# A two-block model on one core: when the S5 state chain, its Toeplitz matrices and the two normalisations run beside the RWKV scan

## The chip, the cores and the metric

One core of a Trainium2 chip runs the whole program. The metric is device time in microseconds (us) of one launch. The names of the engines in the profile are: PE (TensorE, matrix products), DVE (VectorE), ACT (ScalarE), POOL (GpSimd) and SP (SyncE, which here only issues DMA transfers).

## The reference, cut to what matters

The input `x` has 512 tokens of 1024 features. The first block mixes two recurrences, and the change lies in this block only:

```
h = modulate(rms_norm(x), sh_m, sc_m)
proj = h @ w_in[l]                      # z (RWKV columns) and u (S5 columns)
y_rwkv = rwkv7_time_mix(z, ...)         # S = S*w + (S a) b + v k ;  y = S r ; group norm, gate
y_s5 = s5_mix(u, ...)                   # diagonal complex state space, gelu, GLU, rms norm
mix = jnp.concatenate([y_rwkv, y_s5], axis=-1) @ w_out[l]
x = x + g_m[:, None, :] * mix
h = modulate(rms_norm(x), sh_f, sc_f)
x = x + g_f[:, None, :] * ((silu(h @ ffn_w_gate[l]) * (h @ ffn_w_up[l])) @ ffn_w_down[l])
...
```

Inside `s5_mix`, the state of each of 32 groups of 16 channels obeys `s_t = abar * s_(t-1) + bbar u_t`, the output is `Re(C s) + d u`, then `zz = gelu(y)`, `out = zz * sigmoid(zz @ w_glu + b_glu)`, and an rms norm. After this block come two layers of a hybrid of latent attention, short convolution and windowed attention.

## The kernel before, in words

Everything is kept feature-major in SBUF, 128 features by 512 tokens per tile. A dense product takes its weights as blocks of 128x128 in the order in which PE uses them: eight blocks are one unit, 512 KB. SP loads units into a ring of four (`Sync.load`), ACT rounds a unit to its high part (`Scalar.unit`), DVE computes the low part (`Vector.unit`), and PE does three matmuls for each block (`mms`). Two units are split ahead at most. The units of the `ada` product (a vector times a matrix) are used raw from the ring, eight matmuls for four units: SP loads unit u+4 when PE has used unit u (`Sync.whole_done`).

Each engine's program is written by hand as a set of Python generators, one for each strand of the work: `z` (the input projection), `p` (preparation of RWKV), `m` (S5 matrices), `s` (the S5 strand, `s5_apply`), `r` (the RWKV strand), `a` (columns of ada), `g` (group norm) and `o` (first part of the output product). Two strings, `PREP` and `MIX` at the top of the file, set the order: `play` reads a string and takes one step of the named generator for each letter. All engines read the same strings, so a yield that is added to a strand on one engine has to be added on the others. An engine works through its program in order; only semaphores tie the engines together.

The RWKV strand has these steps: token-major v; the grams of `m` and `mt` (two steps); for each of four pairs of chunks p the grams `G` (`grams`) and the token-major b and k; `a` and `kav`; the inverse, five levels of eight steps (four times P: PE 16 matmuls of 64x64, ACT copies; four times T: PE 32 matmuls of 64x64, DVE adds; POOL masks `LL` for the next level); the step matrices (`steps`: four MW, four PR); and eight steps of the scan S0 to S7. In each scan step PE needs the state that DVE scaled in the step before.

The S5 strand has these steps. SP writes u to DRAM and fetches it back with groups on partitions (`UG`). PE computes the local inputs E, ACT copies them to `S`. DVE then runs the state chain: seven steps within blocks of eight (i1 to i7, in `PREP`), seven steps over the block ends (b1 to b7, five operations on 128x32 or 128x16 each), and two steps, called rest 0 and rest 1 here, of four operations on 128x784. The signal `states` stands at their end. SP fetches the Toeplitz matrices `TT` from DRAM with eight DMAs of 256 KB (L3049), PE computes Y in two halves (16 matmuls with `TT` and 32 with `S` each), ACT copies it to `UG`, SP writes it to DRAM with eight DMAs (`scr_yd`, L3056), reads it back as `YS` (L3062) and fetches x once more (L3063). DVE, ACT and DVE again turn `YS` into gelu and its high and low parts (`skip`, `hi`, `lo`), PE computes four `glu` tiles, and the S5 norm gives the rows 4 to 7 of the output product's input (`os`, then `hi` on ACT and `lo` on POOL). Group norm gives rows 0 to 3. `begin_outs` computes a part of the first four output tiles, and `out_one` the rest, 35 us of dense matmuls.

Before the change, the place of the S5 strand is this: b1 to b7 in one step right behind the first grams mask; rest 0 and rest 1 among the grams G0 and G1; the TT fetch on SP behind `states`; the two halves of Y within level 1 of the inverse; `skip` within level 3; `glu` between the steps of the scan; the S5 norm ahead of group norm; and `begin_outs` with rows 4 to 7.

```
for b in range(1, 8):
    step(Sv[:, :, :, b, 7], Sv[:, :, :, b - 1, 7], ...)
yield
...
self.wait_ge(k.s("kpad", 16), "k")
self.wait_ge(k.s("s5_dve"), "states")
for t in range(8):
    self.e.dma_start(k.TT[16 * t:16 * t + 16, :, :], ...)
```

Of the kernel before, what the change touches and what calls it, by code (L numbers as in the profile page):

```python
# [13 lines left out]
T = 512  # L14
# [10 lines left out]
PREP = "zpzzpz" + "smzpm" + "szpmzp" + "ssss" + "zps" + "zpss" + "zpss" + "zps" + "zps"  # L25
MIX = ("rrsrrsrrsrrrsrarrra" + "rrrrrra" + "rrrrsrrsa" + "rrrrrrsa" + "rrrrrrrra" + "rrrsrrrra" + "rrrrrrr" + "rrrrarrrr"
       + "ras" + "rs" * 6 + "r" + "gogoogo")
# [354 lines left out]
class Tensor(Engine):  # L382
# [229 lines left out]
    def s5_apply(self):  # L612
# [16 lines left out]
        for _ in range(11):  # L629
            yield  # L630
        for half in range(2):
            qs = (2 * half, 2 * half + 1)
            ps = [self.take(("yg", q)) for q in qs]
            self.wait_ge(k.s("tt", 16), 7)
            self.wait_ge(k.s("s5_dve"), "states")
            for i in range(8):
                for par in (0, 1):
                    g = 2 * (8 * half + i) + par
                    self.mm(ps[par][:, i * 64:i * 64 + 64], k.TT[:, g, :], k.UG[:, g, :], i == 0, False)
            for i in range(8):  # L640
                for ri in range(2):
# [22 lines left out]
        self.give("s5norm", (act, "ln"))  # L664
        yield
# [49 lines left out]
    def grams(self):  # L715
# [21 lines left out]
        for p in range(4):  # L737
            for which in (0, 1):
# [8 lines left out]
                for hp in (0, 1):  # L747
                    self.give(("g", p, hp, which), (dve, ("g", p, hp, which)))
# [191 lines left out]
    def begin_outs(self):  # L940

        k = self.k
        late = [[(k.s("gn_act"), ("hi", r)), (k.s("gn_pool"), ("lo", r))] for r in range(4, 8)]
        for n in range(4):
            self.begin_out("out", n, k.ysp[4:], range(4, 8), late)
            yield

    def out_one(self):
# [3 lines left out]
        for n in range(8):  # L952
            if n < 4:
                self.dense(("out", n), [("out", n, r) for r in range(4)], k.ysp[:4], k.bank["out", n][:, :], each[:4],
# [291 lines left out]
class Vector(Engine):  # L1246
# [345 lines left out]
    def s5_apply(self):  # L1592
# [4 lines left out]
        yield  # L1597
        for _ in range(4):
# [26 lines left out]
        yield  # L1625
        T = [k.region(110 + 3.125 * i, 16, 7, 7) for i in range(4)]
        ends = [Sv[:, ri, :, 0:7, 7].unsqueeze(3).broadcast_to((128, 16, 7, 7)) for ri in (0, 1)]
        power = lambda ap: ap[:, 0:7, :].rearrange("p i g -> p g i").unsqueeze(2).broadcast_to((128, 16, 7, 7))
        self.wait_ge(k.s("s5_pe"), ("e", 1, 1))
        for ri, op in ((0, ALU.subtract), (1, ALU.add)):  # L1630
            rest = Sv[:, ri, :, 1:8, 0:7]
            V(T[2 * ri], ends[ri], power(k.P8R), ALU.mult)
            V(T[2 * ri + 1], ends[1 - ri], power(k.P8I), ALU.mult)
            self.wait_ge(dve, SOFAR)
            V(rest, rest, T[2 * ri], ALU.add)
            self.wait_ge(dve, SOFAR)
            V(rest, rest, T[2 * ri + 1], op, *(["states"] if ri else []))
            yield
        for _ in range(4):
# [12 lines left out]
        for n in range(4):  # L1652
# [3 lines left out]
            yield  # L1656
        rr = k.rtmp[:, 2, :].rearrange("p (t j) -> p t j", t=8)
# [60 lines left out]
    def grams(self):  # L1718
# [13 lines left out]
        for p in range(4):  # L1732
            for which in (0, 1):
                for hp in (0, 1):
# [3 lines left out]
                    self.tt(part(k.KA if which else k.LT), pv[:, :, 0, :], mask("mSU"), ALU.mult).then_inc(  # L1738
                        *dve.inc(("l", p, hp, which)))
# [374 lines left out]
class Scalar(Engine):  # L2114
# [191 lines left out]
    def s5_apply(self):  # L2306
# [11 lines left out]
        for _ in range(11):  # L2318
            yield
        for q in range(4):  # L2320
            g0 = 16 * (q // 2) + q % 2
# [78 lines left out]
    def rwkv(self):  # L2400
# [16 lines left out]
        self.wait_ge(k.s("prep_dve"), ("bv", 3))  # L2417
        for p in range(4):
            yield
# [324 lines left out]
class Pool(Engine):  # L2744
# [29 lines left out]
    def s5_apply(self):  # L2774
        k = self.k
        for _ in range(2 + 4 + 11 + 2 + 2 + 1 + 4 + 1):
# [6 lines left out]
    def rwkv(self):  # L2783
# [15 lines left out]
        for p in range(4):  # L2799
            self.wait_ge(gdve, ("l", p, 1, 0))  # L2800
# [138 lines left out]
class Sync(Engine):  # L2939
# [90 lines left out]
    def s5_apply(self):  # L3030
# [13 lines left out]
        for _ in range(10):  # L3044
            yield
        self.wait_ge(k.s("kpad", 16), "k")
        self.wait_ge(k.s("s5_dve"), "states")
# [4 lines left out]
        for _ in range(2):  # L3052
# [187 lines left out]
```

## Time and profile before

| | us |
|---|---|
| median of 3 runs | 1702.82 (1700.56 to 1703.16) |
| the profiled execution's own time | 1701.19 |
| its span, first to last instruction | 1699.4 |
| PE busy | 1519.1 (89%), at a mean granted clock of 0.938 |
| DVE busy | 801.0 (47%) |
| ACT busy | 578.9 (34%) |
| POOL busy | 268.3 (16%) |

Busy shares are averages over stages with different limits. In the profile, a wait of an engine is shown as idle time with the engine or transfer that ended it; "issue" means that nothing in the profile ended it. The granted clock is 1.00 at 2.4 GHz and 0.50 at 1.2 GHz.

### The profile page before, as it was taken

How to read it: one execution, taken by the hardware profiler on the slowest of the kernel's cores; microseconds unless marked ns; L12 is line 12 of the kernel's file. 1: busy time of each engine (PE TensorE's matmuls, PEld its weight loads, DVE VectorE, ACT ScalarE, POOL GpSimd, SP SyncE). 2: the span in 40 equal slices, each digit the busy share in tenths (PEclk: the TensorE clock that was granted, in tenths of full speed). 3: DMA queues.
4: the chain of work that ended last, by engine and by line, in shares of the span. 5: the costliest groups of instructions: out<-in, count | busy, mean ns of one | idle time of the engine just before them, and what ended most of it. 6: DMA issues, size and time to landing. Idle time of an engine off the chain costs nothing.

```text
span 1699.4 us, 23751 instructions
## 1 busy us (share of the span) xinstructions
PE 1519.1 (89%) x10024; PEld 1179.0 (69%) x10024; DVE 801.0 (47%) x1264; ACT 578.9 (34%) x996; POOL 268.3 (16%) x224
## 2 busy tenths in 40 slices
PE   6898668788889999999979899988898999998989
PEld 3676548667568888888866687756686677766767
DVE  7666931242554233232345545446634455445552
ACT  4365121123523222222224434224522444222441
POOL 0000312200101011100002233232201232222220
PEclk9999877878889999999989999999998999999999
DMA  9251072731122232332221121111123111211121
GB/s 364 68 121 59 20 127 75 231 145 39 40 72 88 99 98 88 99 130 87 100 88 50 38 75 62 62 50 38 62 88 105 38 54 58 75 62 38 50 87 62
DMA packets 51897, 144.17 MB, mean 85 GB/s; under 512 B 13264, under 2 KB 18000, under 8 KB 51024
## 3 DMA queue, kind: packets, MB, share of 16 engines
q1 hardware_dynamic: 51792, 142.65, 26.1%
q8 instruction: 80, 1.31, 0.3%
q14 instruction: 25, 0.20, 0.0%
HBM read 137.95 MB, written 4.69 MB: 84 GB/s over the span
## 4 chain that ended last, share of the span: by engine, by line
PE 71%; DVE 13%; ACT 8%; issue 4%; DMA 2%; POOL 1%; SPq 1%; DVEq 0%; ACTq 0%
PE b L392 70%; ACT arena L2121 4%; DVE arena L1250 3%; DVE arena L1258 2%; DVE ring L1250 2%; PE b L395 1%; DVE X L1250 1%; ACT ring L2124 1%; POOL arena L2751 1%; DVE arena L1951 1%; DMA ring<-in_ws 1%; ACT L2121 1%; ACT arena L2124 1%; DVE arena L2084 1%; ACT tile L2124 1%
## 5 line engine op out<-in xcount | busy, mean ns | idle before, releaser
L392 PE MATMUL b<-tile,ring 128*128 128x512 f32 x2288 | 705.0, 403 | 9.1 <-DVE ring L1250 5.1
L392 PE MATMUL b<-HR,ring 128*128 128x512 f32 (+1 forms) x1888 | 624.2, 407 | 62.7 <-DVE ring L1250 34.7
L392 PEld LDWEIGHTS b<-tile,ring 128*128 128x128 f32 x2288 | 436.6, 191 | 115.0 <-issue 8.2
L392 PEld LDWEIGHTS b<-HR,ring 128*128 128x128 f32 (+1 forms) x1888 | 364.3, 193 | 164.0 <-issue 61.4
L1250 DVE TENSOR_TENSOR ring<-ring,ring 128x1024 fp32r<-128x1024 f32 x186 | 254.9, 1372 | 299.8 <-ACT ring L2124 295.9
L2124 ACT ACTIVATE ring<-ring 128x1024 fp32r<-128x1024 f32 x186 | 195.7, 1054 | 214.7 <-PE b L392 214.7
L392 PE MATMUL b<-arena 64*64 64x64 f32 (+10 forms) x3072 | 230.8, 290 | 37.9 <-issue 16.7
L392 PEld LDWEIGHTS b<-arena 64*64 64x64 f32 (+5 forms) x3072 | 147.4, 151 | 111.2 <-issue 74.5
L2124 ACT ACTIVATE arena<-b 128x512 f32<-128x512 f32 (+2 forms) x138 | 75.5, 569 | 259.2 <-PE b L392 195.5
L1250 DVE TENSOR_TENSOR arena<-arena 128x512 f32<-128x512 f32 (+7 forms) x194 | 100.3, 549 | 80.0 <-ACT arena L2121 59.1
L2751 POOL TENSOR_SCALAR arena<-arena 128x128 f32<-128x128 f32 (+1 forms) x64 | 87.0, 1378 | 208.9 <-DVE arena L1956 208.9
L2748 POOL TENSOR_TENSOR tile<-arena,tile 128x512 fp32r<-128x512 f32 x38 | 49.8, 1315 | 441.4 <-ACT tile L2124 441.4
L2121 ACT ACTIVATE arena<-arena 128x512 f32<-128x512 f32 (+7 forms) x151 | 72.7, 501 | 84.7 <-DVE arena L1254 46.0
L1250 DVE TENSOR_TENSOR arena<-b,arena 128x512 f32<-128x512 f32 (+3 forms) x78 | 47.8, 629 | 111.9 <-PE b L392 110.6
L2748 POOL TENSOR_TENSOR arena<-arena 128x256 f32<-128x256 f32 (+3 forms) x60 | 64.5, 1098 | 176.3 <-DVE arena L2093 88.3
L395 PE MATMUL b<-cst,arena 128*128 128x128 f32 (+1 forms) x520 | 68.5, 285 | 18.0 <-DVE arena L1250 6.9
L2121 ACT ACTIVATE arena<-b,arena 128x512 f32<-128x512 f32 (+1 forms) x80 | 43.9, 558 | 112.8 <-DVE arena L1254 108.4
L395 PEld LDWEIGHTS b<-cst,arena 128*128 128x128 f32 (+1 forms) x520 | 61.6, 143 | 29.8 <-issue 17.8
L2124 ACT ACTIVATE tile<-arena 128x512 fp32r<-128x512 f32 x58 | 35.2, 628 | 137.9 <-DVE arena L1250 117.5
L1250 DVE TENSOR_TENSOR arena<-arena,b 128x512 f32<-128x512 f32 x52 | 33.5, 681 | 93.1 <-PE b L392 93.0
L392 PE MATMUL b<-ring,HR 128*128 128x512 f32 (+1 forms) x256 | 64.5, 344 | 1.7 <-DVE arena L1261 1.2
L2121 ACT ACTIVATE arena<-b,par 128x512 f32<-128x512 f32 (+1 forms) x58 | 37.5, 685 | 68.2 <-PE b L392 41.4
(112 smaller groups left out, 1024.5 us busy)
## 6 DMA issues: line engine op xcount, KB each, us to landing
ring<-in_ws SPq DMA_DIRECT2D x218, 512.0 KB, 3.5
arena<-in_ws SPq DMA_DIRECT2D x15, 512.0 KB, 15.2
arena<-in_lw SPq DMA_DIRECT2D x2, 1280.0 KB, 5.5
X<-in_xT SPq DMA_DIRECT2D x2, 1024.0 KB, 6.1
arena<-scr_kpad SPq DMA_DIRECT2D x8, 256.0 KB, 11.9
X<-in_xT SPq DMA_DIRECT2D x1, 2048.0 KB, 13.7
outT<-X SPq DMA_DIRECT2D x8, 256.0 KB, 2.0
arena<-in_cst SPq DMA_DIRECT2D x1, 1088.0 KB, 5.1
```

The costliest lines, as they stand in the source:

```text
L392: return self.e.matmul(out, lhsT, rhs, start=start, stop=stop, skip_group_check=True)
L395: return self.e.transpose(out, in_, self.k.C("ident"))
L1250: return self.e.tensor_tensor(out=out, in0=a, in1=b, op=op)
L1258: return self.e.scalar_tensor_tensor(out=out, in0=a, scalar=s, in1=b, op0=op0, op1=op1)
L1951: self.e.tensor_reduce(out=mx[:, q:q + 1], in_=ps[:, o:o + n], op=ALU.max, axis=AX.X).then_inc(*dve.inc((l, "max", h, q)))
L2084: self.e.tensor_reduce(out=mx, in_=Z[:, :, lo:256], op=ALU.max, axis=AX.X).then_inc(*dve.inc((l, "wmax", n)))
L2121: return self.e.activation(out, a, f, scale=scale, **kw)
L2124: return self.e.activation(out, a, ACT.Copy)
L2748: return self.e.tensor_tensor(out=out, in0=a, in1=b, op=op)
L2751: return self.e.tensor_scalar(out=out, in0=a, scalar1=s1, scalar2=None, op0=op0)
```

## The change

It moves steps of the S5 strand and changes no arithmetic. The parts are:

1. SP fetches `TT` right behind E (it waits for `("e", 1, 1)` of PE in the place of `states`), in `PREP`.
2. The block ends b1 to b7 become seven steps of their own, and stand with rest 0 and rest 1 in the levels 1 to 4 of the inverse. Rest 0 and rest 1 use two temporaries at 52 KB in the place of four at 110 KB, which `TT` now fills, so they wait for the last P of level 4.
3. The masking of `LT` on DVE becomes a plain copy on ACT (`gram_act`): the level masks on POOL are strict enough.
4. The two halves of Y move from level 1 of the inverse to the steps PR0 to PR3, each half in two steps (with `TT`, and with `S`).
5. `skip` moves behind scan step S4, `glu` behind S6 and between the steps of group norm, and the S5 norm behind the second step of group norm.
6. `begin_outs` takes the rows 0 to 3 (RWKV), and `os`, `hi` and `lo` of rows 4 to 7 come behind it.
7. The groups of ada stand a little differently among the steps.

```diff
-PREP = "zpzzpz" + "smzpm" + "szpmzp" + "ssss" + "zps" + "zpss" + "zpss" + "zps" + "zps"
-MIX = ("rrsrrsrrsrrrsrarrra" + "rrrrrra" + "rrrrsrrsa" + "rrrrrrsa" + "rrrrrrrra" + "rrrsrrrra" + "rrrrrrr" + "rrrrarrrr"
-       + "ras" + "rs" * 6 + "r" + "gogoogo")
+PREP = "zpzzpz" + "smzpm" + "szpmzp" + "sssss" + "zps" + "zpss" + "zpss" + "zps" + "zps"
+MIX = ("rrrrarrrrarrrrr" + "rrrrrrrra" + "rrsrrsrrrra" + "rrsrrsrrrra" + "rrsrrsrrsrra" + "rrrrsrrsrra"
+       + "rrrrrsrsarsrs" + "rarsrrrsrsrsr" + "sgssgsg" + "oooo" + "s")
...
             ps = [self.take(("yg", q)) for q in qs]
             self.wait_ge(k.s("tt", 16), 7)
-            self.wait_ge(k.s("s5_dve"), "states")
             for i in range(8):
                 for par in (0, 1):
                     g = 2 * (8 * half + i) + par
                     self.mm(ps[par][:, i * 64:i * 64 + 64], k.TT[:, g, :], k.UG[:, g, :], i == 0, False)
+            yield
+            self.wait_ge(k.s("s5_dve"), "states")
...
-        late = [[(k.s("gn_act"), ("hi", r)), (k.s("gn_pool"), ("lo", r))] for r in range(4, 8)]
+        early = [[(k.s("gn_act"), ("hi", r)), (k.s("gn_dve"), ("lo", r))] for r in range(4)]
         for n in range(4):
-            self.begin_out("out", n, k.ysp[4:], range(4, 8), late)
+            self.begin_out("out", n, k.ysp[:4], range(4), early)
             yield
...
-                self.dense(("out", n), [("out", n, r) for r in range(4)], k.ysp[:4], k.bank["out", n][:, :], each[:4],
+                self.dense(("out", n), [("out", n, r) for r in range(4, 8)], k.ysp[4:], k.bank["out", n][:, :], each[4:],
                            start=False)
...
         for b in range(1, 8):
             step(Sv[:, :, :, b, 7], Sv[:, :, :, b - 1, 7], ...)
-        yield
-        T = [k.region(110 + 3.125 * i, 16, 7, 7) for i in range(4)]
+            yield
+        T = [k.region(52 + 3.125 * i, 16, 7, 7) for i in range(2)]
...
-        self.wait_ge(k.s("s5_pe"), ("e", 1, 1))
+        self.wait_ge(k.s("inv_pe"), ("p", 4, 3))
...
-                    self.tt(part(k.KA if which else k.LT), pv[:, :, 0, :], mask("mSU"), ALU.mult).then_inc(
-                        *dve.inc(("l", p, hp, which)))
+                    if which:
+                        self.tt(part(k.KA), pv[:, :, 0, :], mask("mSU"), ALU.mult).then_inc(*dve.inc(("l", p, hp, which)))
...
+            for hp in (0, 1):
+                self.wait_ge(k.s("gram_dve"), ("g", p, hp, 0))
+                self.cp(k.LT[:, p, :].rearrange("p (n a t) -> p n a t", a=2, t=64)[:, :, hp, :],
+                        k.bank["g", p, hp, 0][:, :].rearrange("p (n a t) -> p n a t", a=2, t=64)[:, :, 0, :]).then_inc(
+                    *gram.inc(("l", p, hp)))
...
-            self.wait_ge(gdve, ("l", p, 1, 0))
+            self.wait_ge(k.s("gram_act"), ("l", p, 1))
...
-        for _ in range(10):
-            yield
         self.wait_ge(k.s("kpad", 16), "k")
-        self.wait_ge(k.s("s5_dve"), "states")
+        self.wait_ge(k.s("s5_pe"), ("e", 1, 1))
         for t in range(8):
             self.e.dma_start(k.TT[16 * t:16 * t + 16, :, :], ...)
         yield
-        for _ in range(2):
+        for _ in range(7 + 7 + 2 + 4):
             yield
```

The other lines of the diff only add or drop yields so that the strand keeps step on every engine.

SP's queue from the fetch of `UG` (X<-scr_ud) to the re-read of x. Line numbers grow by 12 to 15 through the change. Before:

```order
17 L3039 DMA X<-scr_ud 16x32x64 x8
18 L2944 DMA ring<-in_ws 128x1024 x6
19 L2983 DMA arena<-in_small 128x512
20 L3049 DMA arena<-scr_kpad 16x32x128 x8
21 L2944 DMA ring<-in_ws 128x1024 x16
22 L3056 DMA scr_yd<-X 16x32x64 x8
23 L3058 DMA arena<-scr_ud 128x4x512
24 L2944 DMA ring<-in_ws 128x1024 x8
25 L3062 DMA arena<-scr_yd 128x4x512
```

And now:

```order
17 L3053 DMA X<-scr_ud 16x32x64 x8
18 L2958 DMA ring<-in_ws 128x1024 x2
19 L3061 DMA arena<-scr_kpad 16x32x128 x8
20 L2958 DMA ring<-in_ws 128x1024 x4
21 L2997 DMA arena<-in_small 128x512
22 L2958 DMA ring<-in_ws 128x1024 x32
23 L3068 DMA scr_yd<-X 16x32x64 x8
24 L3070 DMA arena<-scr_ud 128x4x512
25 L3074 DMA arena<-scr_yd 128x4x512
```

The `TT` fetch (from `scr_kpad`) moved ahead of four weight loads; all loads for ada now stand ahead of the write of `yd`, and none between it and its re-read.

DVE from the last gram masks (arena<-b,cst) into the inverse (adds are arena<-arena,b 128x512, the block ends are the rows with X and 32 or 16 columns). Before:

```order
191 L1250 TENSOR_TENSOR arena<-b,cst 128x4x64 x8
192 L1250 TENSOR_TENSOR arena<-X,arena 128x784 x2
193 L1250 TENSOR_TENSOR X<-X,arena 128x16x7x7 x2
194 L1250 TENSOR_TENSOR arena<-b,cst 128x4x64 x16
195 L1250 TENSOR_TENSOR arena<-arena,b 128x512 x4
196 L1250 TENSOR_TENSOR ada<-b,par 128x8
197 L1250 TENSOR_TENSOR arena<-arena,b 128x512 x12
```

And now:

```order
165 L1253 TENSOR_TENSOR arena<-b,cst 128x4x64 x24
166 L1253 TENSOR_TENSOR arena<-arena,b 128x512 x8
167 L1253 TENSOR_TENSOR ada<-b,par 128x8
168 L1253 TENSOR_TENSOR arena<-X,arena 128x32 x2
169 L1253 TENSOR_TENSOR X<-X,arena 128x32
170 L1253 TENSOR_TENSOR X<-X,arena 128x16 x2
171 L1253 TENSOR_TENSOR arena<-X,arena 128x32 x2
...
193 L1253 TENSOR_TENSOR arena<-arena,b 128x512 x4
194 L1253 TENSOR_TENSOR arena<-X,arena 128x784 x2
195 L1253 TENSOR_TENSOR X<-X,arena 128x16x7x7 x2
196 L1253 TENSOR_TENSOR arena<-arena,b 128x512 x2
```

The masks are now in one piece of 24 instead of 8, 8 and 16, and the block ends and the two rests lie between adds of the inverse.

DVE in the scan (states are arena<-b,nst 128x256), as it now stands:

```order
217 L1253 TENSOR_TENSOR arena<-b,nst 128x256 x4
218 L1261 SCALAR_TENSOR_TENSOR arena<-arena,par 128x512 x4
219 L1253 TENSOR_TENSOR tile_70<-arena,tile_69 128x512
220 L1253 TENSOR_TENSOR tile_72<-arena,tile_71 128x512
221 L1253 TENSOR_TENSOR tile_74<-arena,tile_73 128x512
222 L1253 TENSOR_TENSOR tile_76<-arena,tile_75 128x512
223 L1253 TENSOR_TENSOR arena<-b,nst 128x256
224 L1253 TENSOR_TENSOR ring_55<-ring,ring_55 128x1024 x2
225 L1253 TENSOR_TENSOR arena<-b,nst 128x256
```

`skip` (row 218) and the four `lo` now stand between the states of S4 and S5; before they stood in level 3 of the inverse.

## Rows read from the trace of the kernel before

**Rows 1.** Windows: us, busy us (x instructions) of PE, PEld, DVE, ACT, POOL, PEclk, DMA share, GB/s

```profile
186.10:252.80 66.70, 41.66 (x784) 31.61 (x784) 39.36 (x90) 11.72 (x20) 18.54 (x12) 0.77 0.49 73
252.80:376.60 123.80, 100.61 (x2385) 88.99 (x2388) 33.54 (x59) 26.50 (x45) 20.09 (x16) 0.81 0.44 148
376.60:455.70 79.10, 66.58 (x872) 49.84 (x864) 29.37 (x47) 32.19 (x49) 4.95 (x4) 0.87 0.15 51
455.70:491.20 35.50, 35.38 (x144) 28.07 (x144) 16.97 (x22) 11.58 (x15) 0.00 (x0) 0.95 0.28 90
```

**Rows 2.** Timeline of PE, grams to level 0: start, us, what, count, [idle before <-releaser]

```profile
203.68 1.97 PE L395 MATMUL b<-cst,arena 128*128 128x128 f32 x8 [6.92 <-DVE arena L1250]
...
216.32 1.99 PE L392 MATMUL b<-arena 64*64 64x128 f32 x32 [6.15 <-DVE arena L1250]
...
223.85 1.98 PE L392 MATMUL b<-arena 64*64 64x128 f32 x32 [2.49 <-DVE arena L1250]
...
243.43 1.76 PE L392 MATMUL b<-H,arena 64*64 64x64 f32 x27 [7.24 <-issue]
246.24 6.67 PE L392 MATMUL b<-ring,nst 128*32 128x512 f32 x16 [1.05 <-DMA ring<-in_ws]
```

**Rows 3.** Timeline of POOL (first row) and DVE, 192 to 259 us

```profile
192.25 5.01 POOL L2748 TENSOR_TENSOR arena<-arena,cst 128x512 f32<-128x512 f32 x4 [141.73 <-DVE arena L1250]
...
193.73 3.57 DVE L1250 TENSOR_TENSOR X<-X,arena 128x32 f32<-128x32 f32 x3
...
197.70 0.54 DVE L1250 TENSOR_TENSOR X<-X,arena 128x32 f32<-128x32 f32 x3
...
217.43 2.94 DVE L1250 TENSOR_TENSOR arena<-X,arena 128x784 f32<-128x784 f32 x2
220.39 1.98 DVE L1250 TENSOR_TENSOR X<-X,arena 128x784 f32<-128x784 f32 x2
...
257.80 1.28 DVE L1250 TENSOR_TENSOR arena<-arena,b 128x512 f32<-128x512 f32 x2 [30.13 <-PE b L392]
```

**Rows 4.** Timeline of SP's queue: the TT fetch and the write of yd

```profile
222.46 9.51 SPq L3049 DMA_DIRECT2D arena<-scr_kpad  x8
...
300.16 10.23 SPq L3056 DMA_DIRECT2D scr_yd<-X  x8
```

**Rows 5.** Waits of PE with no releaser, 159 to 456 us: total, times, longest

```profile
PE b L392 <- issue: 27.9, 9, 7.2
```

**Rows 6.** Timeline of PE, Y and two groups of ada

```profile
271.57 14.09 PE L392 MATMUL b<-X,arena 128*128 128x64 f32 x96
...
289.00 7.50 PE L392 MATMUL b<-X,arena 128*128 128x64 f32 x96
296.43 1.94 PE L392 MATMUL b<-ring,nst 128*32 128x512 f32 x16
...
348.46 3.90 PE L392 MATMUL b<-ring,nst 128*32 128x512 f32 x16 [6.01 <-DVE arena L1250]
```

**Rows 7.** Windows around the first half of Y, columns as in rows 1

```profile
271.00:286.00 15.00, 15.00 (x120) 14.70 (x122) 0.00 (x0) 0.89 (x2) 1.27 (x1) 0.52 0.01 2
```

**Rows 8.** Landing of the eight writes of yd (source line L3056)

```profile
DMA to landing us min/median/max: 3.5/5.9/6.5
```

**Rows 9.** Chain that ended last: the re-read of yd (start, us, what)

```profile
331.86 9.43 DMA arena<-scr_yd
```

**Rows 10.** DMA issues on the page: the re-read of x (KB, us to landing)

```profile
X<-in_xT SPq DMA_DIRECT2D x1, 2048.0 KB, 13.7
```

**Rows 11.** Timelines of DVE, PE and POOL: lo, os, group norm's first products, lo of POOL

```profile
345.27 2.50 DVE L1250 TENSOR_TENSOR tile<-arena,tile 128x512 fp32r<-128x512 f32 x4 [1.22 <-ACT tile L2124]
...
421.32 4.00 DVE L1258 SCALAR_TENSOR_TENSOR arena<-arena,par 128x512 f32<-128x512 f32 x4 [6.84 <-ACT arena L2121]
...
427.87 5.76 PE L392 MATMUL b<-arena,cst 128*128 128x512 f32 x8 [1.12 <-ACT arena L2124]
...
426.07 4.95 POOL L2748 TENSOR_TENSOR tile<-arena,tile 128x512 fp32r<-128x512 f32 x4 [92.32 <-ACT tile L2124]
```

More of the change, by code:

```diff
@@ L628, in s5_apply @@
                 yield
-        for _ in range(11):
+        for _ in range(1 + 7 + 7 + 2):
             yield
@@ L747, in grams @@
                 for hp in (0, 1):
-                    self.give(("g", p, hp, which), (dve, ("g", p, hp, which)))
+                    self.give(("g", p, hp, which), (dve, ("g", p, hp, which)),
+                              *([] if which else [(k.s("gram_act"), ("l", p, hp))]))
             yield
@@ L1597, in s5_apply @@
         yield
+        yield
         for _ in range(4):
@@ L1624, in s5_apply @@
                  k.P8I[:, 7, :].unsqueeze(1).broadcast_to((128, 2, 16)), T[0][:, :, :, 0], T[1][:, :, :, 0])
-        yield
-        T = [k.region(110 + 3.125 * i, 16, 7, 7) for i in range(4)]
+            yield
+        T = [k.region(52 + 3.125 * i, 16, 7, 7) for i in range(2)]
         ends = [Sv[:, ri, :, 0:7, 7].unsqueeze(3).broadcast_to((128, 16, 7, 7)) for ri in (0, 1)]
         power = lambda ap: ap[:, 0:7, :].rearrange("p i g -> p g i").unsqueeze(2).broadcast_to((128, 16, 7, 7))
-        self.wait_ge(k.s("s5_pe"), ("e", 1, 1))
+        self.wait_ge(k.s("inv_pe"), ("p", 4, 3))
         for ri, op in ((0, ALU.subtract), (1, ALU.add)):
             rest = Sv[:, ri, :, 1:8, 0:7]
-            V(T[2 * ri], ends[ri], power(k.P8R), ALU.mult)
-            V(T[2 * ri + 1], ends[1 - ri], power(k.P8I), ALU.mult)
             self.wait_ge(dve, SOFAR)
-            V(rest, rest, T[2 * ri], ALU.add)
+            V(T[0], ends[ri], power(k.P8R), ALU.mult)
+            V(T[1], ends[1 - ri], power(k.P8I), ALU.mult)
             self.wait_ge(dve, SOFAR)
-            V(rest, rest, T[2 * ri + 1], op, *(["states"] if ri else []))
+            V(rest, rest, T[0], ALU.add)
+            self.wait_ge(dve, SOFAR)
+            V(rest, rest, T[1], op, *(["states"] if ri else []))
             yield
-        for _ in range(4):
+        for _ in range(4 + 1):
             yield
@@ L1656, in s5_apply @@
             yield
+        yield
         rr = k.rtmp[:, 2, :].rearrange("p (t j) -> p t j", t=8)
@@ L2317, in s5_apply @@
                 yield
-        for _ in range(11):
+        for _ in range(1 + 7 + 7 + 2):
             yield
         for q in range(4):
+            if q % 2 == 0:
+                yield
             g0 = 16 * (q // 2) + q % 2
@@ L2417, in rwkv @@
         self.wait_ge(k.s("prep_dve"), ("bv", 3))
+        gram = k.s("gram_act")
         for p in range(4):
+            for hp in (0, 1):
[3 more added lines that the diff above has]
+                    *gram.inc(("l", p, hp)))
             yield
@@ L2775, in s5_apply @@
         k = self.k
-        for _ in range(2 + 4 + 11 + 2 + 2 + 1 + 4 + 1):
+        for _ in range(2 + 4 + 1 + 7 + 7 + 2 + 4 + 2 + 1 + 4 + 1):
             yield
```

## The prediction

> **What bounds the kernel now.** I read the page first: PE is busy 89% of the span, but the change touches only a part of it, so next came the windows of that part [rows 1]. Behind 491.2 us nothing changes, and ahead of 186.1 us only the fetch of TT moves. Between them PE idles 25.0 us in the grams (66.70 less 41.66), 23.2 us in inverse and step matrices (123.80 less 100.61) and 12.5 us in the scan and group norm. The granted clock is 0.77 to 0.87 there against 0.95 in the dense stage behind, so idle time is paid a second time in slow matmuls.
>
> The timelines tell what ends those waits. In the grams PE waits 6.92, 6.15 and 2.49 us for DVE [rows 2], whose queue holds the block ends and the two rests among the masks [rows 3]. Then it stops for 7.24 us with no releaser, and its next ada weights come late [rows 2]: SP issued the TT fetch only when `states` was there, for 9.51 us [rows 4]. In the whole stretch PE has nine waits with no releaser, 27.9 us [rows 5]; they lie in streams of 64x64 matmuls while DMA moves much data, so I read them as instructions that come late. In the inverse the first half of Y ran 14.09 us and the second 7.50 us for the same 96 records [rows 6], the first at clock 0.52 [rows 7]; and PE waited 6.01 us for `skip`, behind which ada ran 3.90 us in the place of 1.94 us [rows 6].
>
> **Stage 1, 186.1 us to the first P of the inverse (now 252.8).** The block ends, the rests and one third of the masks leave DVE. PE's three waits for it go: -15.6 us. Each pair of chunks now needs six masks on DVE and 2.5 us of grams on PE, so DVE keeps up, but banks come free in turn: I put back 2. The TT fetch leaves: the stop of 7.24 us shrinks to an ordinary one of 3.4 (the other eight average 2.6, the longer ones are 3.4), -3.8; the late weights go, 1.05 of waiting and 6.67 down to 1.94 [rows 2, 6], -5.8. The eight transposes behind the first wait ran at the low clock, 1.97 us [rows 2]; warm they take about half: -0.9. The loads behind the first ada group, which were held back until now, can cost one more stop: +3.4. Sum -20.7, bounds -26 (no added stop, no wait for banks) and -13 (both PE waits come back in half).
> The copy of LT on ACT costs nothing: ACT is busy 11.72 of 66.70 us [rows 1]. If that cover were gone, POOL's level masks would be late, and PE's first P with them.
>
> The TT fetch itself, earlier on, stands ahead of weight loads. SP is taken for 9.51 us and the transfers fill the DMA engines for some 17 to 19 us. A load is wanted four units after it is allowed, each of 24 matmuls of 0.246 us (35.38 / 144 [rows 1]), less some 2.4 us for splitting, so 21 us; 9.5 of it in the queue still leave 11. I cost it at 0; if that cover is gone, it costs PE at most 4 us once.
>
> **Stage 2, to the first scan step (now 376.6).** Y no longer runs cold: its halves should take 7.2 us each in the place of 14.09 and 7.50: -7.2 [rows 6]. The wait for `skip` goes, -6.0, and the cold stretch behind it, -5.5 (ada 2.0, its sums 1.6, the rest of the level 2). The block ends fall where DVE idles: it sat 30.13 us before level 0 [rows 3], and each level leaves it some 3 us and each ada group 2 to 4 more; a step takes 0.9 us (0.54 us [rows 3] for its last three operations, and some 0.4 for the first two). Beside POOL it does not: the three took 3.57 us [rows 3]. I cost them at 0 since they start while PE is at ada; at the other end, seven times 3.0, +21. The rests do cost. They start with the last P; rest 0 takes 4.9 us (2.94 and 1.98 [rows 3]), two adds 1.3, rest 1 4.9, one add 0.7: 11.8 us until the third MW may start, while PE has only T (2.1), ada with its sums (3.9) and two MW (3.5): +2.4. One more us for the Y steps among PR. Sum -15.3, bounds -25 and +6. With stage 1 the scan starts at 376.6 - 36.0 = 340.6 us.
>
> **Stage 3, the scan to the first dense end (now 491.2).** Here the change gives back. The chain of the S5 output starts with the scan and nothing of `glu` can stand in for it. From the start of S0: copies of Y 1.3 us; eight writes of yd, 10.23 us of issue [rows 4] and up to 6.5 to land [rows 8], 16.0; the re-read 0.6 and 7. It took 9.43 behind weight loads [rows 9]; now none stands in front, but x still shares with it (13.7 us [rows 10]); bounds 4 and 13.7. Then `skip`, gelu, hi and lo, 6.4 us (341.31 to 347.7, its last row [rows 11]). That is 31.3 us, and DVE cannot give the state of S5 before, since `skip` stands ahead of it. PE has six scan steps of some 2 to 3 us and one sum, 18 us: **it stands still for about 13 us**. Then S6 and the first glu at the low clock, S7 and the second glu, 11.8; the means 3.7; two glu 6.1; variances 3.6. ACT makes the roots ahead of the last square of the S5 norm, so PE idles 5 and ends that norm at 63.3 us; first gate 0.9, and DVE's four times 2.17 us and one low, so the first row of the output is ready at 72.4 us. As a check: means to first output row took 455.7 - 427.9 = 27.9 us before [rows 11], and take 28.7 here.
> Then the four begun tiles, 12.3 us, to 84.7. Behind the second of them the next unit's split holds DVE until 80.8; `os` 4.00, `hi`, then POOL 4.95 [rows 11] give the last row at 90.7: +4.2. The rest is the 35.4 us of before [rows 1]. Sum 124.3 us against 114.6: +9.7, bounds +2 and +20.
>
> **Sum.** -20.7 - 15.3 + 9.7 = -26.3 us on the profiled execution: 1701.19 - 26.3 = 1674.9. The median of the runs shown lies 1.6 us above that execution, so 1676.5, and I say **1677 us**.
>
> What could speak against it is a rule. The trace shows the stop of 7.24 us inside a stream of matmuls, while 512-byte pieces of TT fill the DMA engines [rows 2, 4]. The Trainium skill (Runtime: NRT & Kernel Launch, section Instruction fetch mechanics) says that instructions are fetched in blocks of 16 KiB while the block before runs, and that this is mostly hidden. If the stop has another cause, it stays, and the sum is 3.8 us smaller: 1681. I go by the row.
>
> **Rivals.**
> *Warm tail (0.20).* The re-read lands in 4 us and the writes of yd, with no weight loads beside them, in 10; the last rows are ready in time; one stop less. That is 3 + 6 + 4 + 3 us more: 1661. For it: nothing else is in the DMA queues. Against: the pieces of yd are 256 bytes.
> *Cold middle (0.24).* Stops of 3.4 us behind every ada group stay [rows 5], and the clock falls behind them and behind the wait for the rests, so that Y keeps its 7.2 us and the levels 5 more, and the block ends meet POOL once: 1677 + 7 + 5 + 3 = 1692. For it: rows 7.
> *Late re-read, slower (0.04).* One mechanism, at DVE's `skip` between the states of S4 and S5: everything behind it moves one for one with the landing of the re-read. It lands 24.9 us after S0 starts by my sum; the gain is used up at 24.9 + 26 = 51 us. The nearest rows reach that only if all queue up: weight loads of ada 14, writes of yd 16.7, x ahead of the re-read 13.7 and the re-read itself 9.4, 54 us: 1706. Against it: SP waits for yd before it issues either, and issues the re-read first.
> *No change (0.02).* The two gains only move PE's idle time to the wait in the scan.
>
> **How the numbers follow.** My forecast (1677, give or take 7) has 0.50. The range reaches to the centres of both neighbours: 1661 to 1693. About 0.2% (3.4 us) is what a measurement of this kernel can tell from no change; faster by more than that holds for the forecast and the first two rivals, 0.94; the same 0.02; slower 0.04.
>
> **What would show it.** Right: no wait of PE over 3 us for DVE between 190 us and the first P, which starts near 232; SP's TT fetch near 139 us, with no longer wait of PE for ring rows between 140 and 165; Y in four pieces at clock 1.00, 14 to 15 us in all; S0 near 341; a single wait of PE of 10 to 16 us in the scan, ended by DVE's state of S5, with the landing of the re-read ahead of it; and dense matmuls to the end from about 425. Wrong: Y at 20 us or more; waits of PE for DVE within the levels 1 to 3, next to slow operations on 128x32; or a wait in the scan over 25 us.

## The result and the profile after

The changed kernel takes 1654.88 us (median of 4 runs, 1654.14 to 1660.91) against 1701.69 (4 runs, 1700.43 to 1703.16): ratio 0.9732, 95% interval 0.9707 to 0.9757. Beside a later batch it took 1655.36 (6 runs), ratio 0.9721 (0.9697 to 0.9744). The direction was right, the size was not: forecast 1677, range 1661 to 1693.

Windows of the changed kernel, cut at the same places of the program as [rows 1]: grams, first P to S0, S0 to the last dense product of the output, the rest (us, then busy us and instructions of PE, PEld, DVE, ACT, POOL, then PEclk, DMA share, GB/s):

```profile
185.58:219.50 33.92, 32.73 (x784) 26.29 (x786) 16.92 (x39) 14.70 (x29) 14.93 (x12) 0.95 0.36 128
219.50:318.60 99.10, 85.65 (x2395) 73.89 (x2390) 51.84 (x100) 19.06 (x33) 20.05 (x16) 0.97 0.36 130
318.60:445.14 126.54, 106.28 (x1010) 81.83 (x1008) 50.54 (x67) 50.68 (x74) 4.97 (x4) 0.84 0.29 88
445.14:1659.00 1213.86, 1127.37 (x4984) 873.31 (x4984) 548.40 (x794) 410.30 (x748) 223.46 (x182) 0.96 0.22 72
```

| stage | before | after | difference | forecast |
|---|---|---|---|---|
| 1, grams | 66.70 | 33.92 | -32.8 | -20.7 |
| 2, first P to S0 | 123.80 | 99.10 | -24.7 | -15.3 |
| 3, S0 to the last dense product | 114.60 | 126.54 | +11.9 | +9.7 |

The rest took 1208.20 us before; its instructions are unchanged, and the profiled execution (1660.91 us) lies 6 us above the kernel's other three, so the last row is no part of the change.

PE in the grams: the waits for DVE and the stop of 7.24 us of [rows 2] are gone, and the 128 matmuls of `kav` (fifth row) run in one piece. The first group of ada takes 1.94 us, the second 4.30: its weights still arrive a little late (PE's own weight loads wait for `ring<-in_ws` twice within it), and with thin weights, below, it takes 1.95. Timeline (start, us, what, [idle before <-releaser]):

```profile
193.68 2.56 PE L392 MATMUL b<-arena 64*64 64x64 f32 x103 [1.19 <-issue]
196.17 1.94 PE L392 MATMUL b<-ring,nst 128*32 128x512 f32 x16
...
203.91 4.30 PE L392 MATMUL b<-ring,nst 128*32 128x512 f32 x16
...
212.09 3.71 PE L392 MATMUL b<-cst,arena 128*64 128x128 f32 x64
215.73 3.95 PE L392 MATMUL b<-H,arena 64*64 64x64 f32 x128
```

DVE: the last three operations of a block end, alone and beside POOL's masks, and the second rest (two multiplies, two adds):

```profile
233.51 0.54 DVE L1253 TENSOR_TENSOR X<-X,arena 128x32 f32<-128x32 f32 x3
...
234.45 3.58 DVE L1253 TENSOR_TENSOR X<-X,arena 128x32 f32<-128x32 f32 x3
...
287.69 2.98 DVE L1253 TENSOR_TENSOR arena<-X,arena 128x784 f32<-128x784 f32 x2
290.70 1.99 DVE L1253 TENSOR_TENSOR X<-X,arena 128x784 f32<-128x784 f32 x2
```

PE around the rests and Y: no wait for DVE stands in front of the MW at 290.47, and Y is four pieces of 3.79 us (the first two shown), 15.2 in all for the 21.6 of [rows 6]:

```profile
285.64 1.15 PE L392 MATMUL b<-arena 64*64 64x64 f32 x32 [1.47 <-issue]
286.72 1.94 PE L392 MATMUL b<-ring,nst 128*32 128x512 f32 x16
288.60 1.95 PE L392 MATMUL b<-cst,H 128*128 128x1 f32 x16
290.47 8.32 PE L392 MATMUL b<-arena 64*64 64x128 f32 x160
...
303.48 3.79 PE L392 MATMUL b<-X,arena 64*128 64x63 f32 x64
```

The S5 output chain (SP's queue; two pieces of the chain that ended last: the end of the last write and the re-read; DVE), then PE from the end of the scan: the state of S5, the first glu, the last square of the S5 norm, the gates, the begun tiles and the rest of the output:

```profile
319.80 8.04 SPq L3068 DMA_DIRECT2D scr_yd<-X  x8
...
326.53 4.15 DMA scr_yd<-X
...
330.70 8.22 DMA arena<-scr_yd
...
338.95 2.74 DVE L1261 SCALAR_TENSOR_TENSOR arena<-arena,par 128x512 f32<-128x512 f32 x4 [5.82 <-DMA arena<-scr_yd]
```

```profile
345.79 1.65 PE L392 MATMUL b<-arena 64*64 64x64 f32 x26 [1.41 <-DVE arena L1253]
349.40 4.67 PE L392 MATMUL b<-tile,ring 128*128 128x512 f32 x12
...
379.54 2.08 PE L392 MATMUL b<-arena,cst 128*128 128x512 f32 x2 [6.63 <-ACT arena L2127]
381.41 4.74 PE L392 MATMUL b<-arena 128*128 128x512 f32 x8
391.38 14.14 PE L392 MATMUL b<-tile,ring 128*128 128x512 f32 x48 [5.24 <-ACT tile L2130]
408.67 36.45 PE L392 MATMUL b<-tile,ring 128*128 128x512 f32 x144 [3.15 <-POOL tile L2762]
```

### The profile page after: what moved, and what is told of

Its sections match the earlier page's. It is cut to its first block, busy times and chain, and to the rows that moved or that the text cites. A ratio compares the mean times of both kernels' runs of the same rounds, so it can differ in the third digit from the quotient of the medians.

```text
span 1659.0 us, 23756 instructions
## 1 busy us (share of the span) xinstructions
PE 1502.9 (91%) x10024; PEld 1164.8 (70%) x10024; DVE 801.2 (48%) x1256; ACT 581.5 (35%) x1004; POOL 264.3 (16%) x224
## 3 DMA queue, kind: packets, MB, share of 16 engines
q8 instruction: 80, 1.31, 0.3%
## 4 chain that ended last, share of the span: by engine, by line
PE 73%; DVE 12%; ACT 8%; issue 4%; POOL 1%; DMA 1%; SPq 0%; DVEq 0%; ACTq 0%
PE b L392 72%; ACT arena L2127 5%; DVE arena L1261 2%; DVE ring L1253 2%; DVE arena L1253 2%; PE b L395 1%; ACT ring L2130 1%; POOL arena L2765 1%; DVE arena L1957 1%; DVE arena L2090 1%; ACT arena L2130 1%; ACT L2127 1%; DVE arena L1915 1%; ACT tile L2130 1%; DMA cst<-in_cst 1%
## 5 line engine op out<-in xcount | busy, mean ns | idle before, releaser
L392 PE MATMUL b<-tile,ring 128*128 128x512 f32 x2288 | 709.9, 405 | 13.5 <-ACT tile L2130 5.2
L2127 ACT ACTIVATE arena<-b 128x512 f32<-128x512 f32 (+1 forms) x44 | 24.7, 561 | 84.3 <-PE b L392 84.3
## 6 DMA issues: line engine op xcount, KB each, us to landing
arena<-in_ws SPq DMA_DIRECT2D x15, 512.0 KB, 15.2
arena<-scr_kpad SPq DMA_DIRECT2D x8, 256.0 KB, 11.8
X<-in_xT SPq DMA_DIRECT2D x1, 2048.0 KB, 12.7
```

What stands on the lines that cost most here:

```text
L392: return self.e.matmul(out, lhsT, rhs, start=start, stop=stop, skip_group_check=True)
L2127: return self.e.activation(out, a, f, scale=scale, **kw)
```

## The experiments

Each difference below is a median against the changed kernel's 1654.9 or 1655.4 us; ratios are against the kernel before, timed beside each batch. The changed kernel itself ran only beside three of them (thin weights, both tail edits, the tail's old order). The kernel before had medians from 1701.7 to 1704.9 us in these batches, so a difference of 3 to 5 us of the other runs is not clear of noise by the times alone; there the rows of the trace carry the reading.

### Which part of stage 1 gives what

**TT alone**: the kernel before with the `TT` fetch behind E; the rests' temporaries go to `H`, since `TT` fills theirs.

```diff
-        for _ in range(10):
-            yield
         self.wait_ge(k.s("kpad", 16), "k")
-        self.wait_ge(k.s("s5_dve"), "states")
+        self.wait_ge(k.s("s5_pe"), ("e", 1, 1))
         for t in range(8):
             self.e.dma_start(k.TT[16 * t:16 * t + 16, :, :], ...)
         yield
+        for _ in range(10):
+            yield
```

> The kernel before with one part of the change alone: SP fetches TT behind E (the two rests use two temporaries elsewhere, so nothing else moves). Theory W (my prediction's terms: a stop shrinks to an ordinary one of 3.4 us, the ada weights come in time): -3.8 - 5.8 = -9.6 us against before, so 1692. Theory C (a stop without a releaser is caused wholly by the transfer beside it and goes wholly, and the clock behind it stays high): -7.2 - 5.8 - 1 or more, so 1688 or less. Rival N (the fetch was hidden, or it takes the time again where it now lies, among the weight loads of the projection): 1699 or more.

Measured: 1688.35, ratio 0.9927 (0.9890 to 0.9964), 14 us faster, as theory C has it. The first P (the first product of the inverse) stands at 239.31 us for 252.84. PE's waits for DVE remain (7.12, 6.30 and 2.59 us); `kav` runs unbroken and ada behind it in 2.09 us:

```profile
229.66 3.71 PE L392 MATMUL b<-cst,arena 128*64 128x128 f32 x64
233.30 4.06 PE L392 MATMUL b<-H,arena 64*64 64x64 f32 x128
237.29 2.09 PE L392 MATMUL b<-ring,nst 128*32 128x512 f32 x16
239.31 3.89 PE L392 MATMUL b<-arena,ring2f 64*64 64x64 f32 x126
```

So the stop of 7.24 us went as a whole, not down to 3.4. Of the later ones the next, in level 0, is longer here, 2.58 us for 1.46. The stage from the first transposes to the first P, columns as in the windows above:

```profile
186.31:239.31 53.00, 35.94 (x785) 29.66 (x785) 39.54 (x90) 11.73 (x20) 17.58 (x12) 0.81 0.12 42
```

This run moves the stop and the late weights together and does not price the stop alone. In the kernel before, the chain that ended last runs between 225 and 246 us from SP's issue of TT over the weights of ada queued behind it, and not through the stop:

```profile
232.02 14.17 DMA ring<-in_ws
```

These weights were there only at 246.2 us. With the stop alone gone, PE would have waited for them as long.

**Block ends back**: the changed kernel with b1 to b7 and both rests among the grams again (the letters of `MIX` moved, temporaries in `H`).

> The changed kernel with the block ends and the two rests back among the grams on DVE (temporaries in a free place), all else as changed. Theory W: PE gets back its waits of 6.9, 6.2 and 2.5 us and nothing else, +15.6 against the changed kernel, so 1670.5. Theory C: beside these waits the clock falls, which makes the matmuls of the grams some 5 us longer, so 1675 or more. Rival I (in the inverse they cost time as well, beside POOL): under +12, so under 1667.

Measured: 1667.90, ratio 0.9793 (0.9753 to 0.9833), +13.0, between theory W and rival I. First P at 233.14 for 219.50. The waits are not those of the kernel before: 6.99, 3.16 and 0.79 us, with the copies of `LT` on ACT. The first two:

```profile
203.60 3.66 PE L392 MATMUL b<-ring,nst 128*32 128x512 f32 x16 [6.99 <-DVE arena L1253]
...
215.45 2.90 PE L392 MATMUL b<-arena 64*64 64x128 f32 x64 [3.16 <-ACT arena L2130]
```

**TT among the grams**: the changed kernel with the fetch between the loads for two groups of ada.

> The changed kernel with the TT fetch put back among the grams, behind the masks of G0 and ahead of the loads for the next ada group. Theory W: a stop of 3.8 us and late weights of 5.8 us come back, +9.6, so 1664.5. Theory C: the whole stop of about 7 us and the late weights, and cold matmuls behind both, so 1668 or more. Rival N: no difference from the changed kernel, 1655.

Measured: 1671.08, ratio 0.9812 (0.9772 to 0.9853), +16.2. The first P came at 238.62 us. Beyond the stop of 0.95 us at their start PE has none among the grams; the price is all in weights that came late (PE, then SP's queue):

```profile
220.71 6.59 PE L392 MATMUL b<-ring,nst 128*32 128x512 f32 x16 [17.06 <-DMA ring<-in_ws]
```

```profile
197.59 9.88 SPq L3047 DMA_DIRECT2D arena<-scr_kpad  x8
207.52 20.25 SPq L2958 DMA_DIRECT2D ring<-in_ws  x8
```

**LT back on DVE**: the changed kernel with both masks of a gram on DVE.

> The changed kernel with the masking of LT back on DVE in the place of the copy on ACT: eight operations of 0.33 to 0.41 us more on DVE in the grams, eight copies less on ACT. Theory W and C: DVE has idle time of 0.6 to 4.9 us between the pairs of chunks, so within 1 us of the changed kernel, 1655. Rival B (banks come free later and PE waits for them): +2 to +3 us, 1657 to 1658.

Measured: 1655.75, ratio 0.9722 (0.9682 to 0.9762): nothing, once the block ends have left DVE.

### What the stops are

**Thin weights**: 28 loads of ada's weights cut to 64 KB, so that these columns of ada are computed from weights that were not loaded.

```diff
-            self.load(u + RING)
+            v = u + RING
+            if 38 <= v < 66:
+                k = self.k
+                self.e.dma_start(k.wraw(v)[:, 0:128], k.d["ws"][v, :, 0:128])...
+            else:
+                self.load(v)
```

> The changed kernel with 28 of the 32 weight loads for ada in the inverse and the step matrices cut to an eighth of their bytes (64 KB in the place of 512). The instructions of all engines stay as they are; those columns of ada are computed from weights that were not loaded, so its output isn't the reference's. It asks where the stops of PE with no releaser come from that the prediction counted on (2.58 to 4.4 us each there; in the changed kernel eight of 1.2 to 2.1 us, 13.4 in all, stand in the inverse). Theory D (they come from the transfers' traffic: instructions arrive late because the DMA engines carry weights): the stops go down below 3 us in all, and the time by 9 to 12 us, to 1643 to 1646. Rival I (they belong to the instruction stream itself, some fixed number of instructions apart): stops of 13 us stay, time unchanged within 1.5 us.

Measured: 1647.64, ratio 0.9662 (0.9639 to 0.9685), -7.7. Between the two theories: PE's stops fall from 18.4 to 12.3 us (waits of PE, total, times, longest), those of stage 2 from 13.4 to 7.8. The second fence is the changed kernel:

```profile
PE b L392 <- issue: 12.3, 10, 1.9
```

```profile
PE b L392 <- issue: 18.4, 11, 3.0
```

Traffic makes the stops longer, but most of their time stays with an eighth of it. I then counted the matmul records between neighbouring stops: in the kernel before 509, 253, 254, 507, 253, 129 and 381; in the changed one 885, 254, 129, 254, 129, 382, 127, 253, 1019, 128. All are multiples of 128 within three or, at 885, eleven records (a trace can miss some). Two of the windows between stops (PE first; last the clock, the DMA share and GB/s). Behind each PE stops again (1.52 and 1.62 us), with a DMA share of 0.02:

```profile
239.41:243.02 3.61, 2.09 (x129) 1.95 (x128) 2.48 (x4) 0.00 (x0) 0.00 (x0) 1.00 0.02 5
...
271.63:275.34 3.71, 2.09 (x127) 1.99 (x127) 3.12 (x9) 0.00 (x0) 0.00 (x0) 1.00 0.02 4
```

**A shift of the stream**: 64 matmul records more ahead of the grams.

```diff
-                    ins = self.quads(p, gram)
+                    for _ in range(2 + 1 if (name, p) == ("m", 0) else 1):
+                        ins = self.quads(p, gram)
```

A first try with four extra repeats told nothing apart:

> The changed kernel with the 16 matmuls of the first quarter of the product m issued four times more, so 64 more matmuls of 64x64 (1.1 us of PE) stand ahead of the grams; nothing is left out. It asks what the stops of PE with no releaser are. In the kernel before and in the changed one, and in every run since, the matmuls between two neighbouring stops are 127 to 130, 253 or 254, 381 or 382, 507 to 509, 885, 1018 or 1019: whole multiples of 128 matmuls, which with their weight loads are 256 instructions; and the page has an instruction queue of 80 packets with 1.31 MB, 16 KB each, for 10024 matmuls and as many weight loads. Theory F (a stop is the fetch of the next block of 256 instructions that comes late): the stops stand 64 matmuls earlier in the program. Those that stood 50, 85, 105, 13 and 32 matmuls ahead of a group of ada then stand 114, 149 or 21, 169 or 41, 77 and 96 ahead. The distances stay multiples of 128. Rival L (they belong to places in the program, a semaphore or a bank): they stay 50, 85, 105, 13 and 32 ahead. Time by both: within 4 us of 1655.4.

It made 128 records more, not 64 (10152 for 10024), and the stops stood 50, 85, 105, 13 and 32 records ahead of ada as before, as both theories then have it; 81 packets of instructions for 80; 1659.56 us. The same on the fastest kernel (both tail edits, below, at 1644.42): 1647.86. With two repeats:

> The shift again, by half a block. The run with 16 matmul calls issued four times more (e13_shift64) shows 10152 matmul records for 10024, since a call with float32 operands makes two; it shifted the stream by 128 records, a whole multiple, and could not tell the theories apart: both expect the stops where they were, and there they stood (50, 85, 105, 13 and 32 records ahead of ada), with 81 packets of instructions for 80. Here the 16 calls are issued twice more: 64 records. Theory F (a late block of 128 matmuls and their weight loads): the stops stand 64 records earlier in the program, so that 114, 149 or 21, 169 or 41, 77 and 96 records follow up to ada in the place of 50, 85, 105, 13 and 32. Rival L (places in the program): they stay. Time: within 4 us of 1655.4.

Measured: 1658.65, ratio 0.9735 (0.9712 to 0.9759). The stops moved as theory F (late blocks of the instruction stream) has it, to 113, 22, 169, 76 and 95 records ahead of ada. Three of them, and behind them the first two in the changed kernel (the third is the row at 285.64 us, shown above, with 32):

```profile
230.19 1.90 PE L392 MATMUL b<-arena 64*64 64x64 f32 x113 [0.88 <-issue]
...
276.96 1.38 PE L392 MATMUL b<-arena 64*64 64x64 f32 x76 [1.80 <-issue]
...
287.02 3.01 PE L392 MATMUL b<-arena 64*64 64x64 f32 x95 [2.11 <-issue]
```

```profile
228.31 0.97 PE L392 MATMUL b<-arena 64*64 64x64 f32 x50 [1.69 <-issue]
...
275.34 0.45 PE L392 MATMUL b<-arena 64*64 64x64 f32 x13 [1.62 <-issue]
```

The fastest kernel with 96 records more (three repeats) had them 18, 54, 73, 108 and 0 records ahead, as 96 records ask, at 1648.61 us. So the stops follow the instruction stream and not places in the program: they are late blocks of 128 matmuls with their weight loads.

### The tail

**Square early**: `gated_square(3)` on ACT right behind the last sigmoid.

```diff
             if n:
                 self.gated_square(n - 1)
+            if n == 3:
+                self.gated_square(3)
             yield
-        self.gated_square(3)
```

> The changed kernel with the last square of the S5 norm taken by ACT right behind the last sigmoid, ahead of group norm's roots. In the changed kernel PE waits 6.63 us for that square, then at the gates 5.24 us. Theory P (the part of the prediction on the S5 norm): the square itself is what is late; the 6.63 us wait goes down to 1 to 2 us, the roots behind it start 0.5 us later, the first output row moves forward by about 4 us: about 1650.8 us. Rival R: the path is group norm's root chain (ACT roots, DVE reciprocals), and the S5 norm only stands beside it: PE's wait moves to the gates and grows there to 10 us, time unchanged at 1654.9.

Measured: 1651.52, ratio 0.9698 (0.9667 to 0.9728), -3.4, near theory P; the interval overlaps that of the changed kernel. The wait of 6.63 us is gone, the next grew from 5.24 to 10.62, and the begun tiles start 4.0 us earlier:

```profile
387.42 14.20 PE L392 MATMUL b<-tile,ring 128*128 128x512 f32 x48 [10.62 <-ACT tile L2130]
```

**os in the middle**: `"oooo" + "s"` becomes `"oo" + "s" + "oo"`.

> The changed kernel with os, hi and lo of rows 4 to 7 one step earlier, behind the second begun output tile and ahead of the split of the unit that comes then. The prediction charged 4.2 us because this split holds DVE, and the changed kernel shows a wait of PE of 3.15 us for POOL's last row behind the begun tiles. Theory P: the wait goes, and the split is still in time: about 1651.7 us. Rival R: the last rows depend on the S5 norm and not on DVE's place in the queue, or the split comes late in their place and PE waits as long for DVE: 1654.9.

Measured: 1649.87, ratio 0.9693 (0.9663 to 0.9723), -5.0, with an interval that overlaps too. Begun tiles and the rest are one piece of 47.68 us; they were 14.14, a wait of 3.15 and 36.45:

```profile
396.37 47.68 PE L392 MATMUL b<-tile,ring 128*128 128x512 f32 x192 [5.33 <-ACT tile L2130]
```

**Y first**: `"rrrrrsrsarsrs"` becomes `"rrrrssssrrarr"`.

> The changed kernel with all four steps of Y together between the MW and the PR steps, and the PR steps and ada behind them, so that the write of yd and the skip chain start earlier against the scan. The prediction read the stage behind S0 as bound by that chain (yd, re-read, skip, hi, lo), at PE by a wait of some 13 us; measured were waits of 5.2 us in all beside slow matmuls at clock 0.50 to 0.69. Theory P (the chain binds): Y ends about 6 us earlier and the first output row with it, since the PR and ada work then fills the hole at full clock; the time falls by 4 to 6 us, to about 1650. Rival R (the chain is not the bound, PE's slow clock is): PE loses as much ahead of S0 as it gains behind, 1654 to 1656. Rival Q (DVE's rests are late): the second half of Y waits for the rests, which end just 11.9 us behind the last P; PE waits 2 to 4 us there and the gain shrinks to 1 or 2 us.

Measured: 1656.43, ratio 0.9723 (0.9693 to 0.9753), no gain. The writes of yd start at 318.81 us for 319.80, although Y ended 5.6 us earlier (313.04 for 318.64) and ACT had copied it by 314.16: in SP's queue the loads that wait for the last group of ada now stand in front. So the chain moved by 1 us only, and this run does not test what 5 us would do. The wait for DVE's state of S5 is 0.24 us for 1.41, and the first glu starts at 350.03.

**x late**: SP waits for `ys` ahead of the fetch of x.

> The changed kernel with the second fetch of x held back on SP until the re-read of yd has landed. In the changed kernel x is issued right behind it; yd's re-read takes 8.2 us and x 12.7 us. Theory P (they share the DMA engines): alone the re-read, half the size of x, lands in 4 to 5 us, skip and everything behind it come 3.5 us earlier, about 1651.5 us. Rival R: what comes earlier meets PE still in the scan steps, so only the wait gets shorter and the time falls by 1 us at most. Rival Q: the re-read takes 8 us by itself (small pieces, latency), no change.

Measured: 1658.58, ratio 0.9740 (0.9710 to 0.9770), no gain. The re-read of yd takes 7.7 us by itself (8.2 with x beside it):

```profile
arena<-scr_yd SPq DMA_DIRECT2D x1, 1024.0 KB, 7.7
```

**Both tail edits**:

> The changed kernel with both edits that helped one by one: the last square of the S5 norm ahead of group norm's roots (1651.5 alone, 3.4 us below the changed kernel), and os, hi and lo of rows 4 to 7 behind the second begun tile (1649.9 alone, 5.0 below). Theory P: they act at two places of one path and add up: 1646.5 us. Rival R: with the begun tiles 4 us earlier the S5 norm is no longer early enough for the last rows and the wait for POOL comes back: 1649.

Measured: 1644.42 (1643.11 to 1648.84), ratio 0.9651 (0.9627 to 0.9674): 10.9 us below the changed kernel beside it, clear of noise, and the fastest of all. The single gains add up to 8.4; why it is more is not shown. Begun tiles and the rest are one piece of 47.80 us from 390.59.

**Old order of the tail**: the S5 norm ahead of group norm, rows 4 to 7 begun (`"sssss" + "gogoogo"`, with `begin_outs` and `out_one` as before).

> The changed kernel with parts 5 and 6 of the change undone in the tail alone: glu and the S5 norm ahead of group norm, the begun tiles with rows 4 to 7 and between the steps of group norm, rows 0 to 3 last. Theory G (the new order gives back time): in the kernel before, the stretch from group norm's first products to the last product took 63.3 us, since the begun tiles fill group norm's waits, and in the changed one 87.6 us with 14.6 us of glu and squares in it, 73 without; with the old order the last product ends some 5 to 9 us earlier: 1646 to 1650. Rival H (the new order pays, since the S5 chain is late): the begun tiles wait for os, hi and POOL's lo, which start only behind the S5 norm's root at about 373 us, DVE's os stands ahead of group norm's products, and the last product ends 3 to 8 us later: 1658 to 1663.

Measured: 1649.74 (1643.33 to 1654.08), ratio 0.9670 (0.9645 to 0.9695), 5.6 below the changed kernel. Dense work now lies between the steps of group norm; what is left of waits is POOL's last row and one for DVE:

```profile
381.18 5.05 PE L392 MATMUL b<-tile,ring 128*128 128x512 f32 x12 [5.53 <-POOL tile L2762]
...
405.54 35.39 PE L392 MATMUL b<-tile,ring 128*128 128x512 f32 x144 [4.01 <-DVE tile L1253]
```

## Why the prediction was wrong

**Stage 1, forecast -20.7, measured -32.8: the step that failed is the pricing of PE's stops and waits that I kept or added.** Three such terms never came: the stop of 7.24 us "shrinks to an ordinary one of 3.4" (it went as a whole), "one more stop: +3.4", and "I put back 2" for banks. They make 8.8 of the 12.1 us. The TT-alone run shows the first two without the rest of the change: the first P came 13.5 us earlier, and 7.24 of stop and 5.8 of late weights make 13.0. The other 3.3 us are matmul time: PE busy fell by 8.9 us and I had counted 5.6; the granted clock went from 0.77 to 0.95. It fell by more than counted although the second group of ada still ran 4.30 us for the forecast 1.94. The DVE terms were too small even without the +2: -15.6 and -0.9 make 16.5, and from the TT-alone run to the changed kernel the stage fell by 19.1 us (53.00 to 33.92), 16.0 of it waits for DVE and 3.2 matmul time. Putting the block ends back cost only 13.0 (13.6 at the first P); there the masks of `LT` stay off DVE, and no run has both back without TT.

Why the terms were wrong: I took the usual length of a stop as a fixed price. They are late blocks of 128 matmuls. In the levels a block of 64x64 matmuls runs in 2.1 us and the next one was there after 3.6 to 3.7 us (the windows 239.41 and 271.63), so PE stops for some 1.6 us each time. In the grams of the changed kernel 784 matmuls are 6.1 blocks in 33.9 us, 5.5 us each; the one stop, 1.19 us, stands ahead of the loads and was there before (1.20), and behind it 885 records run without one. In the kernel before, the 7.24 us stood behind TT: from 228 to 244 us the DMA view of that kernel has one packet of instructions, while the data packets (q1) took 124% of 16 engines' span, more than their full time; the second fence is the changed kernel from 219 to 318 us, 19 packets:

```profile
q1 hardware_dynamic: 3135, 1.72, 124.2%
q8 instruction: 1, 0.02, 0.8%
```

```profile
q1 hardware_dynamic: 3456, 12.58, 34.6%
q8 instruction: 19, 0.31, 1.3%
```

The rule that I set against the row, the Trainium skill (Runtime: NRT & Kernel Launch, section Instruction fetch mechanics), describes these blocks: 16 KiB, 256 instructions. The trace agrees: 80 packets and 1.31 MB for 20,048 records, and the stops 128 matmuls and as many weight loads apart. Its "mostly hidden" does not hold in these streams: 18.4 us of stops remain. So I was right to go by the row, and right that instructions come late. What the forecast lacked was how long a block runs against how long the next one takes to be there. The kernel before had one such row: a block ran in 2.10 us and the next was there after 6.19 (317.45 to 323.64 us).

**Stage 2, forecast -15.3, measured -24.7.** Y at full clock (1.00 in all four pieces), the wait for `skip` and the cold stretch behind it came as forecast. The step "the rests do cost, +2.4", and 1 more for Y, failed: the third MW might start 11.9 us behind the last P (forecast 11.8), but PE took as long itself, with a T of 4 us in the place of 2.1 and a stop of 1.47 us. That the stop filled this place is luck. With thin weights PE is earlier there, and the wait appears:

```profile
285.05 5.46 PE L392 MATMUL b<-arena 64*64 64x128 f32 x112 [1.67 <-DVE arena L1253]
```

The stops fell from 17.2 to 13.4 us, where I had left them alone. These two make 7.1 of the 9.4 us; the rest is clock (PE busy -15.0, counted -12.7). Block ends beside POOL did slow down, to 3.58, 2.44 and 1.64 us, and PE never waited for them. No run undid the moves of Y and `skip` alone, so their shares are read from the rows, not shown by an experiment.

**Stage 3, forecast +9.7, measured +11.9.** The first row of the output came 72.8 us behind S0 (forecast 72.4). That match is luck, since the picture of a 13 us stand in the scan was wrong: yd landed 10.9 us after its first write, not 16 (the terms 10.23 and 6.5 make 16.7), so PE could go on with the state of S5 27.2 us behind S0 for 31.3. Of the 13 us some 4 fell away with that, some 4 were slow matmuls (22 us of work for 18), 3.8 were stops and 1.41 the wait for DVE. One window there, at clock 0.50:

```profile
336.00:345.80 9.80, 7.57 (x168) 7.19 (x168) 5.64 (x10) 7.64 (x13) 0.00 (x0) 0.50 0.57 238
```

So x late gained nothing; Y first did not get the chain away early enough to tell. The begun tiles took 14.14 us (12.3), and `os`, `hi` and `lo` cost 3.15 (4.2).
**The TT fetch in the projection** cost nothing, as forecast: SP issued it from 138.31 us for 9.28 us, and PE's two waits for ring rows stayed 5.45 and 2.72 us (before: 5.45 and 2.70).

**Rivals.** *Warm tail* had 1661 and half of its reasons (yd in 10.9 us, one stop less); *cold middle* was refuted by Y's four pieces at clock 1.00. 1661 came nearest, but for other reasons than the ones that decided: it has none of the missed terms of stage 1 but one stop. *Late re-read* and *no change* did not come about. The range left out that several kept costs could fail together.

## What to carry to other kernels

Count PE's waits without a releaser in matmuls, not in microseconds: if the distances are multiples of 128, they are late instructions, and what counts is how long 128 matmuls run there. Look for what a transfer that fills the DMA engines holds up: here TT (2 MB in 512-byte pieces) delayed the weights queued behind it, and in the kernel before the instructions too, which cost 14 to 16 us among the grams and nothing in the projection. A chain that moves late can take the filler of other waits with it: the tail's old order, or an order in which each engine's late work stands ahead of its long work, gave back 5.6 to 10.9 us here.

## What was not expected of the hardware

A block of 128 short matmuls and their weight loads runs in 2.1 us, but where such blocks stop one after another the next one comes 3.6 to 3.8 us after the one before in the changed kernel (3.61, 3.71, 3.83), and 3.34 us after it at the least in the other runs (TT among the grams, and the first shift on the fastest kernel). Cutting the weight traffic left 3.72 and 3.82 us there, and took away 5.6 us of stops elsewhere. So both are there: a delay of its own, and contention on top of it. What sets the delay is not shown. The re-read of yd, 1 MB, takes 7.7 us alone and 8.2 beside 2 MB of x. One matmul call with float32 operands of 64x64 makes two records in the profile: 64 calls more made 128 records more (10152 for 10024), and 32 calls 64.
